# Two layers of a hybrid model on one core: where the delta layer's norms, its first weights and the expert rows are handled

## The reference, cut to what matters

```python
y = hierarchical_moe(h, ...)              # two experts a token, weights w_tok
x = x + gt2[:, None, :] * y
x = rmsnorm(x, g_final)                   # ends the first block

h = x                                     # second block
h = h + deltanet_mixer(rmsnorm_2(h, a_norm), a_w_in, a_conv_w, ...)

def deltanet_mixer(h, w_in, conv_w, ...):
    p = h @ w_in                          # 1024 -> 3*1024 (q, k, v) + 1024 (gate) + 16 (beta, a)
    qkv, gate, b_raw, a_raw = split(p)
    qkv = silu(causal_dwconv_2(qkv, conv_w))     # 4 taps
    q, k = l2norm(q) * 128 ** -0.5, l2norm(k)    # per head
    ...                                   # chunked gated delta rule
    o = rmsnorm_2(o, onorm_g) * silu(gate)
    return o @ w_out

def rmsnorm(x, g):
    return x * rsqrt(mean(x * x) + 1e-6) * g
```

## Time and profile before

| | us |
|---|---|
| three runs | 2506.64, 2506.78, 2511.77 (median 2506.78) |
| profiled execution, its time | 2503.68 |
| its span | 2502.0 |
| TensorE matmul busy | 2284.3 (91%) |
| VectorE busy | 1193.9 (48%) |
| ScalarE busy | 813.4 (33%) |
| GpSimd busy | 119.5 (5%) |
| mean granted TensorE clock | 0.953 |

### The profile page before, as it was taken

The page is one execution under the profiler, slowest core; times in us unless marked ns, Lnnn a source line. Parts: engine busy times, 40 slices in busy tenths (PEclk is TensorE's granted clock), DMA queues, the critical chain, the costliest instruction groups (busy, mean ns, idle before and its releaser), DMA issues.

```text
span 2502.0 us, 29684 instructions
## 1 busy us (share of the span) xinstructions
PE 2284.3 (91%) x11716; PEld 1572.7 (63%) x11716; DVE 1193.9 (48%) x1734; ACT 813.4 (33%) x1250; POOL 119.5 (5%) x160
## 2 busy tenths in 40 slices
PE   7999989499999999749987689999999889999997
PEld 3788657233333333228767677888787777888775
DVE  4899584300000000056556544777724473777832
ACT  4222542211111111143464154232324274223312
POOL 0000000111111111100003000000000000000000
PEclk9999999799999999979989599999999899999999
DMA  9442105359999999511210002222222301222221
GB/s 370 159 168 101 68 29 240 138 234 382 373 376 390 404 379 384 217 79 68 89 71 10 1 35 72 97 101 101 101 101 71 131 1 68 101 101 93 76 101 67
DMA packets 36405, 384.54 MB, mean 154 GB/s; under 512 B 10080, under 2 KB 10336, under 8 KB 13408
## 3 DMA queue, kind: packets, MB, share of 16 engines
q1 hardware_dynamic: 27520, 374.91, 38.3%
q0 software_dynamic: 8800, 8.45, 1.0%
HBM read 384.10 MB, written 16.83 MB: 160 GB/s over the span
## 4 chain that ended last, share of the span: by engine, by line
PE 62%; DVE 12%; ACT 4%; issue 2%; DMA 1%; POOL 0%; DVEq 0%; SPq 0%; ACTq 0%; POOLq 0%
PE PS L591 11%; PE PS L592 11%; PE PS L593 11%; PE PS L793 9%; PE PS L832 4%; PE PS L813 4%; PE PS L840 2%; DVE A L1757 2%; DVE ring_r L2041 2%; PE PS L557 2%; ACT w_hi_r L1380 1%; DVE hid_r L2264 1%; PE PS L946 1%; DVE A L1752 1%; PE PS L783 1%
## 5 line engine op out<-in xcount | busy, mean ns | idle before, releaser
L592 PE MATMUL PS<-h_r,w_hi_r 128*128 128x512 f32 x1104 | 432.3, 392 | 0.0
L591 PE MATMUL PS<-h_hi_r,w_hi_r 128*128 128x512 f32 x1056 | 418.2, 396 | 10.5 <-ACT A L1407 7.2
L593 PE MATMUL PS<-h_hi_r,ring_r 128*128 128x512 f32 x1056 | 413.3, 391 | 0.0
L2041 DVE TENSOR_TENSOR ring_r<-ring,w_hi_r 128x1024 fp32r<-128x1024 f32 x196 | 238.6, 1223 | 361.4 <-ACT w_hi_r L1380 361.4
L1380 ACT ACTIVATE w_hi_r<-ring 128x1024 fp32r<-128x1024 f32 x196 | 202.6, 1051 | 331.5 <-PE PS L593 206.2
L591 PEld LDWEIGHTS PS<-h_hi_r,w_hi_r 128*128 128x128 f32 x1056 | 199.7, 189 | 62.5 <-issue 17.3
L592 PEld LDWEIGHTS PS<-h_r,w_hi_r 128*128 128x128 f32 x1104 | 209.1, 189 | 44.8 <-issue 1.9
L593 PEld LDWEIGHTS PS<-h_hi_r,ring_r 128*128 128x128 f32 x1056 | 199.5, 189 | 42.3
L2017 DVE TENSOR_TENSOR A<-A,PS 128x512 f32<-128x512 f32 x16 | 11.0, 688 | 395.1 <-PE PS L793 395.1
L793 PE MATMUL PS<-A 128*64 128x512 f32 x768 | 169.1, 596 | 0.1
L592 PE MATMUL PS<-hid_r,w_hi_r 128*128 128x512 f32 x352 | 138.3, 393 | 0.0
(11 more groups left out here) (451 smaller groups left out, 3739.2 us busy)
## 6 DMA issues: line engine op xcount, KB each, us to landing
A<-wexp SPq DMA_DIRECT2D x64, 2048.0 KB, 9.7
ring<-wall SPq DMA_DIRECT2D x63, 2048.0 KB, 8.1
ring<-wexp SPq DMA_DIRECT2D x16, 2048.0 KB, 17.9
h<-wexp SPq DMA_DIRECT2D x16, 2048.0 KB, 13.3
A<-wada SPq DMA_DIRECT2D x12, 2048.0 KB, 15.4
x<-xt_in SPq DMA_DIRECT2D x2, 2048.0 KB, 11.3
A<-y_assignments SPq DMA_DIRECT2D x4, 1024.0 KB, 8.0
h_tokens<-A SPq DMA_DIRECT2D x4, 512.0 KB, 2.8
```

Source lines behind the costliest of these rows:

```text
L591: mm(out, w[0], x_[0], start=first, stop=False)
L592: mm(out, w[0], x_[1], start=False, stop=False)
L593: return mm(out, w[1], x_[0], start=False, stop=last_)
L2041: tt(ring_r[:, slot, :, cols], ring[:, slot, :, cols], w_hi_r[:, :, cols].bitcast(F32), ALU.subtract).then_inc(S("w_lo"), 1)
```

## The change

1. Loads: after the last expert silu SyncE issues the ab weights and the delta layer's first two weight units, then waits for the scatters and issues the four loads of y rows, each with a semaphore of its own (`to_A{t}`, which four loads at the start use too).
2. Rows: VectorE waits for each block by itself before it sums it, and TensorE transposes block by block (t outermost).
3. Weights: ScalarE and VectorE split the first unit and the ab weights before the rows.
4. Norms: the product's input is x times the two gains (`gm[:, 0]` = g_final x a_norm), unnormed. The factor of both norms, the product of two rstd values per token (`token_scale`, A's tile 23), is multiplied in when a tile leaves PSUM: one more VectorE operation for each tile, into `z`, from which the convolution reads. The gate tiles are multiplied on VectorE and then get their silu on ScalarE from SBUF. The ab rows are multiplied too.
5. Sums of norms 2 and 3: all eight squares in A, eight matmuls of 32 columns in four column groups, a copy, and one matmul of the total; they stand between tiles 0 to 5. Norm 2 still rewrites x, now beside tiles 2 and 3.
6. ScalarE's roundings are issued one tile further ahead of silu (piece m + 5 in step m from m = 8 on), with the first ones set by hand; VectorE's splits of pieces 9 to 12 are moved too.

The core of the diff (waits and orders; declarations and renamings left out):

```diff
+            rwait(sp, S("m_sg"), 4 * n)
+            sp.dma_start(wab[:], w_ab).then_inc(S("small2"), 16)
+            for u in range(NU1, NU1 + 2):
+                sp.dma_start(ring[:, u % 2], wall[u]).then_inc(S(f"unit{u % 2}"), 16)
             for j in range(2):
                 rwait(sp, S(f"sc{j}"), 32 * n + 16 * NT)
...
-                sp.dma_start(A[:, 4 * t:4 * t + 4, :], y_asg.rearrange("(t p c) d -> t p (c d)", p=P, c=2)[t]).then_inc(S("y2"), 16)
-            for u in range(NU1, NU1 + 2):
-                sp.dma_start(ring[:, u % 2], wall[u]).then_inc(S(f"unit{u % 2}"), 16)
-            sp.dma_start(wab[:], w_ab).then_inc(S("small2"), 16)
+                sp.dma_start(A[:, 4 * t:4 * t + 4, :], y_asg.rearrange("(t p c) d -> t p (c d)", p=P, c=2)[t]).then_inc(S(f"to_A{t}"), 16)
...
# TensorE
+            def norm_quarters(n):
+                for k in range(KD):
+                    g = QUARTER * (k % 4)
+                    pe.wait_ge(S("sq"), sq_count(n) + k + 1)
+                    last = mm(PS[g:g + QUARTER, NORM_BANK[n], :], ones[:, 0:QUARTER], A[:, k, :], start=k < 4, stop=k >= 4)
+                last.then_inc(S("sq_used"), 1)
+            def norm_total(n):
+                pe.wait_ge(S("sq"), sq_count(n + 1))
+                mm(PS[:, NORM_BANK[n], :], ones, sq[:, 0, :], start=True, stop=True).then_inc(S("sq_used"), 1)
...
             for t in range(NT):
                 pe.wait_ge(S("y_sum"), t + 1)
-            for k in range(KD):
-                for t in range(NT):
+                for k in range(KD):
                     last = nc.tensor.transpose(PS[:, k, t * P:(t + 1) * P], A[:, 16 + 2 * t + k // 4, (k % 4) * P:(k % 4 + 1) * P], ident)
-            norm(2, 0)
...
-            norm(3, 0)
-            wait_split(1)
+            a_tile(0)
             for k in range(KD):
                 last = product(PS[0:2 * DH, 4, :], (wab_hi[:, k, :], wab_lo[:, k, :]), h_split(k), k == 0, k == KD - 1)
             last.then_inc(S("ab_mm"), 1)
-            sgroup(G_AIN, h_split)
+            norm_quarters(2)
+            a_tile(1)
+            norm_total(2)
+            a_tile(2)
+            a_tile(3)
+            norm_quarters(3)
             pe.wait_ge(S("ab_ev"), 1)
+            a_tile(4)
+            norm_total(3)
+            a_tile(5)
+            pe.wait_ge(S("ab_ev"), 2)
             for t in range(NT):
                 last = nc.tensor.transpose(PS[:, 7, 16 * t:16 * t + 16], ab_rows[:, t * P:(t + 1) * P], ident[0:2 * DH, 0:2 * DH])
             last.then_inc(S("ab_mm"), 1)
+            pe.wait_ge(S("std"), 4)
+            a_tile(6)
+            pe.wait_ge(S("ab_ev"), 3)
+            a_tile(7)
+            for g in range(2, 8):
...
# ScalarE
+            for k in range(KD):
+                act.wait_ge(S("xt"), KD + k + 1)
+                a_(h_hi_r[:, k, :], x[:, k, :], ACT.Identity, scale=gm[:, 0, k:k + 1]).then_inc(S("h_hi"), 1)
+            norm(2, (4, 5))
+            w_hi(NU1 + 1, 2)
+            norm(3, (7, 8))
...
-                w_hi(NU1 + 1 + m // 4, m % 4)
+                for p in ([9] if m == 0 else [8 + m // 2 + 1] if m in (2, 4, 6) else [m + 5] if 8 <= m < 23 else []):
+                    w_hi(NU1 + p // 4, p % 4)
...
# VectorE
+            for j in range(4):
+                w_lo(NU1, j)
+            dve.wait_ge(S("small2"), 112)
...
             for t in range(NT):
+                dve.wait_ge(S(f"to_A{t}"), 96 if t < 2 else 32)
...
             for k in range(KD):
                 dve.wait_ge(S("yT"), k + 1)
                 stt(x[:, k, :], PS[:, k, :], mod[:, 40 + k:41 + k], x[:, k, :], ALU.mult, ALU.add).then_inc(S("xt"), 1)
+                if k:
+                    dve.wait_ge(S("xt"), KD + k)
+                    a_lo(k - 1)
...
+            w_lo(NU1 + 1, 0)
             dve.wait_ge(S("ab_mm"), 1)
             cp(ab_rows, PS[0:2 * DH, 4, :]).then_inc(S("ab_ev"), 1)
+            w_lo(NU1 + 1, 1)
+            norm(2, V("g_final", 0, KD), x, "xt")
+            w_lo(NU1 + 1, 2)
+            w_lo(NU1 + 1, 3)
+            w_lo(NU1 + 2, 0)
+            dve.wait_ge(S("std"), 4)
+            link(tt(token_scale, token_scale, rstd[:], ALU.mult))
+            tt(ab_rows, ab_rows, token_scale[0:2 * DH, :], ALU.mult).then_inc(S("ab_ev"), 1)
             for m in range(24):
...
-                w_lo(NU1 + 1 + m // 4, m % 4)
+                for p in ([9 + m // 2] if m in (1, 3, 5, 7) else [m + 4] if m > 8 else []):
+                    w_lo(NU1 + p // 4, p % 4)
                 dve.wait_ge(S("mm"), TILE_DONE[g][m % 4])
...
-                src = PS[:, 4 * (g % 2) + m % 4, :]
-                conv(dst, src, 4, lambda j: V("a_conv_w", 24 * j + m), None).then_inc(S("ev_dve"), 1)
+                z = A[:, 16 + m % 2, :]
+                link(tt(z, PS[:, 4 * (g % 2) + m % 4, :], token_scale, ALU.mult))
+                conv(dst, z, 4, lambda j: V("a_conv_w", 24 * j + m), None).then_inc(S("ev_dve"), 1)
```

More of the change, by code:

```diff
@@ L91 @@
           + [(["w_out0"], "X"), (["w_out1"], "X")]
-          + [([f"a_in{i}"], "D" if i < 6 else "A") for i in range(8)] + [(["a_out0"], "X"), (["a_out1"], "X")]
+          + [([f"a_in{i}"], "D") for i in range(8)] + [(["a_out0"], "X"), (["a_out1"], "X")]
           + [([f"up0_{i}"], "D") for i in range(FU)] + [([f"down0_{3 * m + i}" for i in range(3)], "X") for m in range(2)]
@@ L130, in tile_done, with sq_count, used_count @@
     return UNIT_USED[UNITS[NU1 - 1]] + 4 * (u - NU1) + j + 1
+GROUPED = (2, 3)
+def sq_count(n):
+    return sum(KD + 1 if i in GROUPED else KD for i in range(n))
+def used_count(n):
+    return sum(2 if i in GROUPED else KD for i in range(n))
 def split_count(u, j):
@@ L278, in build @@
         g_last = ab[:, :, 0:DH]
+        token_scale = A[:, 23, :]
         moe_up, moe_dn = [A[:, 0:8], A[:, 32:40]], [A[:, 24:32], h[:]]
@@ L379, in ada_sem @@
         def ada_sem(a):
-            return f"ada{a if a < 4 else a % 2}"
+            return f"to_A{a if a < 4 else a % 2}"
         def ada_sums(a):
@@ L916, in _ @@
             last.then_inc(S("ab_mm"), 1)
-            for g in range(1, 8):
-                sgroup(G_AIN + g, h_split, sums=4 * (g - 2) if 2 <= g < 6 else None, emptied=4 * (g - 3) if 3 <= g < 7 else None)
+            pe.wait_ge(S("std"), 4)
[3 more added lines that the diff above has]
+            for g in range(2, 8):
+                sgroup(G_AIN + g, h_split, sums=4 * (g - 2) if g < 6 else None, emptied=4 * (g - 3) if 3 <= g < 7 else None)
             freed(pe, G_AIN + 6)
@@ L1186, in inv_sqrt, with norm @@
                 return a_(dst, dst, ACT.Exp, scale=-0.5)
-            def norm(n):
+            def norm(n, between=()):
                 for k in range(KD):
@@ L1193, in norm @@
                         act.wait_ge(S("xt"), KD * (n - 1) + k + 1)
-                    if KD * n + k >= 2:
-                        act.wait_ge(S("sq_used"), KD * n + k - 1)
-                    a_(sq[:, k % 2, :], x[:, k, :], ACT.Square).then_inc(S("sq"), 1)
-                act.wait_ge(S("sq_used"), KD * (n + 1))
-                bank = NORM_BANK[n]
-                inv_sqrt(rstd[:], PS[:, bank, :], 0, 1.0 / D).then_inc(S("std"), 1)
+                    if k >= 2 and n not in GROUPED:
+                        act.wait_ge(S("sq_used"), used_count(n) + k - 1)
+                    a_(A[:, k, :] if n in GROUPED else sq[:, k % 2, :], x[:, k, :], ACT.Square).then_inc(S("sq"), 1)
+                if n in GROUPED:
+                    act.wait_ge(S("sq_used"), used_count(n) + 1)
+                    a_(sq[:, 0, :], PS[:, NORM_BANK[n], :], ACT.Copy).then_inc(S("sq"), 1)
+                for m in between:
+                    w_hi(NU1 + m // 4, m % 4)
+                act.wait_ge(S("sq_used"), used_count(n + 1))
+                inv_sqrt(token_scale if n == 3 else rstd[:], PS[:, NORM_BANK[n], :], 0, 1.0 / (QUARTER * D if n in GROUPED else D)).then_inc(S("std"), 1)
             act.wait_ge(S("small"), 32)
@@ L1370, in _ @@
                     last.then_inc(S("m_y1"), 1)
-            norm(2)
             def w_hi(u, j, load_count=None, free_count=None, slot=None):
@@ L1395, in x_hi @@
                     a_(dst[:, k, :], x[:, k, :], ACT.Identity, scale=V(gain_name, first + k)).then_inc(S("h_hi"), 1)
-            norm(3)
             for j in range(4):
                 w_hi(NU1, j)
-            h_hi("h", KD * 3)
+            for k in range(KD):
+                act.wait_ge(S("xt"), KD + k + 1)
[3 more added lines that the diff above has]
+            norm(3, (7, 8))
             def sum_out(i):
@@ L2010, in _ @@
             nc.vector.memset(A[HALF:P, 48, :], 0.0)
+            link(tt(gm[:, 0, :], V("g_final", 0, KD), V("a_norm", 0, KD), ALU.mult))
             n = doubles(dve)
@@ L2109, in _ @@
                 tt(A[:, i, :], A[:, i, :], l_sum[i], ALU.mult).then_inc(S("l_n"), 1)
+            for i in range(4, 8):
+                gate(i)
             def per_head(v, n=DH):
```

70 lines of the change are left out of this document (40 added, 30 removed).

## The result

The changed kernel took 2478.76 us (median of 4 runs, 2471.44 to 2482.93) against 2508.61 for the kernel before in the same runs: ratio 0.9877, 95% interval 0.985 to 0.9904, so 29.9 us or 1.2% faster. In five further rounds it took 2471.39 against 2506.34, ratio 0.9868 (0.9847 to 0.9889), 35.0 us. The forecast was 2473.7 in a range of 2463 to 2487.

The account below looks back on a forecast made before the run. The prediction saw a serial start, saturated TensorE, then 14.7 us lost, mostly to ScalarE's Ln and Exp queue; -21.2 - 12.3 + 0.4 = -33.1 on 2503.7 gave 2470.6, as median 2473.7 us, range 2463 to 2487.

Parts of the forecast that it names:

- The sum: Whole kernel: -21.2 - 12.3 + 0.4 = -33.1 us on the profiled 2503.7, giving 2470.6, or 2473.7 as the runs' median.
- Part 1: Rows combined block by block as loads land, first x update at 1068.5 instead of 1075.03: -6.5 us.
- Rival C: At the row loads: blocks land together or the wait for weights shows; price 6 us, 2480; chance 0.07.
- Part 2: First weights split under the row loads: hidden; at most 4.6 us would come back if the cover failed.
- Part 3: Norms out of the product's input, from tile 0 to the second sum: second sum at 1159.7 against 1180.86, -21.2 us.
- Part 4: Roundings ahead of silu, second to sixteenth sum: 91.4 us instead of 103.75, -12.3.
- Rival A: Second to sixteenth sum: the Ln and Exp stall stays whole; price 12.3 us, 2486; chance 0.13.
- Part 5: End of the input projection: eight tiles as before, later last silu +0.3, routing multiply +0.1, delayed roundings nothing; +0.4 us.
- Rivals B: The two TensorE gaps before tile 8 and the first sum are absent or cost half: 6 to 12 us better; chance 0.1.
- D: TensorE stays at 1.2 GHz from tile 0 to past the fourth tile after the second sum: 2524 us; chance 0.03.
- E: Partial form of D's low clock, some 5 to 10 us: 2479 to 2484; chance 0.09.
- The two rules beside the rows: Skill's drains at ScalarE table loads (6.9 us more for five switches) and TensorE tiling changes; rows bound each below 0.1 us.

Follow-up runs that it names:

- E2: Changed kernel, but VectorE waits for all four row loads before summing the first block: stage 253.7 us against 247.0, median 2479.39.
- E3: Changed kernel, but the first unit's four weight pieces are rounded and split after the rows, loads still early: stage 254.4 us against 247.0, median 2478.72.
- E1: Changed kernel with ScalarE's roundings from piece 13 on back in their old place: stage 262.7 us against 247.0, median 2487.17.
- E11: Kernel before with only ScalarE's roundings issued earlier, ahead of silu: stage 268.8 us against 281.6, median 2496.25 against 2506.03.
- E10: Changed kernel with E9's edits, splits of pieces 9 to 11 later and the gate block in step 12: stage 232.0 us against 247.0, median 2456.65.
- E5: Changed kernel with the sums of norms 2 and 3 as eight full 128-column matmuls each: stage 255.8 us against 247.0, median 2489.5.
- E9: Changed kernel with squares 0 and 1 in step 3, later squares one step earlier, sums copied ahead of silu: stage 235.9 us against 247.0, median 2466.55.
- E7: Changed kernel with ScalarE's squares 0 and 1 issued in step 3 instead of 6 and 7: stage 241.0 us against 247.0, median 2467.81.
- E8: E7 with VectorE's splits of pieces 9 and 10 moved behind convolution 3, and 11 to step 6: stage 237.3 us against E7's 241.0, median 2462.55.

## Why the prediction was right, point by point

- **The sum.** -33.1 was forecast for the profiled execution, the stage gave -34.5. The medians gave -29.9 and -35.0, so how near a single median comes to the forecast is in part chance. Each term of the sum is within 1.0 us of what it measured.
- **Part 1** (-6.5): the first x update stands 19.04 us behind the start of the stage (1070.20 - 1051.16) against 25.99 before: -6.95, and E2 takes 6.1 of it back. Rival C is out by the four landings, and by ScalarE, which began the four roundings at 1052.26, right behind its last copy, with the weights there since 1046.96.
- **Part 2** (hidden): VectorE finished its splits at 1058.4 and the first block landed 1.9 later. What the prediction priced too low is the loss if the cover fails: it gave "at most the 4.6 us", E3 lost 7.4, since TensorE then starts only behind the first split and VectorE's alternation no longer hides tile 0.
- **Part 3** (second sum 21.2 earlier): 110.0 us behind the start of the stage against 131.8, so -21.8. The steps held: the wait for unit 2's load, the third of the layer (the first rounding of it ran to 1116.4, predicted 1114.6), the token scale at 1121.0 (predicted 1119.3), both in a trace that is 2.1 late as a whole, gaps of 5.00 and 5.50 where 5.6 and 6.6 were forecast, each released by the engine named. The clock loss was 2.7 for the tile behind the second gap's sum (9.0 us instead of 6.3), where I took 2. Two errors offset each other here: the first sum came 1.25 us earlier than forecast (1152.17 less 2.12, against 1151.3), and what follows up to the second sum took 9.0 us against 8.4, which gave 0.6 back. The convolution was mis-sized by 0.17 us, 3.48 instead of 3.65 (from one row of its first multiply to the next, 1126.61 to 1130.09): its first step takes 0.49 us here, not the 0.55 of the earlier trace rows.
- **Part 4** (-12.3): 91.64 against the forecast 91.4, with waits of 1.09 and 1.33 for the square and the copy where 0.9 and 1.5 were worked out. E1 and E11 give 12.35 and 12.1 for this part from both sides. Rival A is out.
- **Part 5** (+0.4): -0.6. In the kernel before, the last eight tiles were not quite without gaps, as the text has it: TensorE waited 0.41 us at 1296.95 for a sum copy, and that is gone; and E1 shows that this part depends on the roundings as well (3.1 us), which "nothing" left out. E11, with the roundings alone, has the same -0.7, so it is their doing, and the extra multiply ahead of the last silu cost 0.1 and not 0.4.
- **Rivals B, D and E**: neither gap was absent, and from the ab product to the token scale the granted clock was 1.00. Tile 0, fed one product at a time, ran at 0.55 from 1073 to 1076 and at full clock from there on.
- **The two rules beside the rows.** After: Ln, Exp and their two table loads took 1096.74 to 1100.67, 3.93 us, each beginning 0.01 to 0.02 us behind the one ahead, so with no drain between them, as in the earlier trace rows. The Trainium skill ("ScalarE: Activation LUTs", What ACT_TABLE_LOAD costs) would have 2.8 more, an estimate from the page. The quarter sums of norm 3 started 0.32 us behind the 128-column product ahead of them, where the pitch is 0.23 (1106.96 to 1107.28), which is 0.1 us more, the bound that the prediction took. By the Trainium skill ("TensorEngine Tiling (Array Packing)", Key Properties) a change of tiling mode drains the engine; at most these 0.1 us can be that.

Two things are left open. No run undoes the folding of the norms by itself. E11 and the changed kernel differ by 21.8 us of the stage, which is the worth of parts 1, 2 and 3 together; of these, E2 and E3 show the rows and the splits (6.7 and 7.4, which may overlap), and what the folding adds is read from the traces. And there is the scatter of the runs, which lies outside the stage (last section).

## What to carry to other kernels

On an engine that works strictly in order, an instruction that others wait for should stand ahead of one that itself waits: issuing each rounding one tile earlier, ahead of a silu, gave 12 us, in either kernel; moving two squares gave 5.9 more, and moving the other squares and the copies 5.1 on top. When a factor is folded from a product's input into its eviction, everything that is evicted queues behind the factor; ask which buffer fills first, and take all work out of that path that can wait (two splits of 1.2 us gave 2.3 at the wait that they stood in). Preparing an operand under a transfer can be worth more than its own duration (7.4 us for splits of 4.6) where it lets the next engine follow piece by piece.

## What the runs showed of the hardware that I had not expected

**The stretch ahead of the stage scatters in steps, with TensorE's clock.** It took 1048.6 to 1060.3 us in executions whose work there is the same but for one instruction. The modulation's column sums, TensorE timelines of the changed kernel in its first profiled execution, then in its second, then of E10:

```profile
25.71 1.05 PE L606 MATMUL PS<-cst,A 128*128 128x1 f32 x8 [1.45 <-ACT A L1254]
...
30.01 1.87 PE L606 MATMUL PS<-cst,A 128*128 128x1 f32 x8 [0.70 <-ACT A L1254]
...
35.82 1.05 PE L606 MATMUL PS<-cst,A 128*128 128x1 f32 x8 [0.73 <-ACT A L1254]
```

```profile
26.31 1.05 PE L606 MATMUL PS<-cst,A 128*128 128x1 f32 x8 [1.45 <-ACT A L1254]
...
29.93 1.05 PE L606 MATMUL PS<-cst,A 128*128 128x1 f32 x8 [0.72 <-ACT A L1254]
```

```profile
30.45 1.87 PE L606 MATMUL PS<-cst,A 128*128 128x1 f32 x8 [0.70 <-ACT A L1254]
...
36.61 1.87 PE L606 MATMUL PS<-cst,A 128*128 128x1 f32 x8 [0.72 <-ACT A L1254]
```

A group takes 1.05 us or 1.87 (granted clock 1.00 or 0.50), and the next group starts 3.6 us behind a fast one where the clock stays up, 4.3 to 5.3 behind it where the clock falls on the way, and 5.8 to 6.2 behind a slow one: short bursts of matmuls with pauses of 0.7 us run at either level of the clock, and which one differs from execution to execution. In E10 the profiled execution took 2468.25 and the five others 2455.18 to 2460.46; it had 11.6 us more ahead of the stage than the second one of the changed kernel. The first 96 us hold 5.6 of them. The other 6.0 lie between 300 and 515 us, and the profiled executions of E5 and E9 lose the same 5.9 there, in the same steps; around the first of these steps the granted clock was 0.85 in E10 (306 to 329 us) and 1.00 in the changed kernel's second execution (300 to 320). Such steps are about as large as the 5 us by which the two median gains of the changed kernel differ. Whether a kernel's code shifts the odds is open.

**Behind the stage full clock was the slower case.** To the end of the span it took 1171.1 to 1171.5 us in six of the fourteen profiled executions and 1172.3 to 1175.5 in the other eight. In the six, the granted clock was 0.54 to 0.62 in a stretch 26 to 30 us behind the end of the stage; GpSimd's multiply, which waits for TensorE, began at 31.5, and a small copy on VectorE took 0.16 us at 30.8. In the eight the clock was 1.00 there, so that GpSimd began at 29.9. The same copy then took 1.46 us and ended 0.03 behind GpSimd's operation (32.26 and 32.23), and TensorE's wait for the VectorE operation behind it was 3.64 us instead of 0.70. That the copy is held up by GpSimd's operation fits all fourteen, but no run moves one of the two. The wait's end moves by 1.3 us; the rest of the 1 to 4 us is not placed.

**Behind a gap.** Tile 8 took 8.1 to 8.2 us after waits of 4.98 and 5.00 us (E7 and the changed kernel's first profiled execution), 7.2 after 4.97 (E9), 7.2 after 2.72 (E8) and 5.6 after 2.73 (E10): a gap costs up to 2.7 us more than its own length, and two equal gaps need not cost the same.
